# Step sizes at the head of the sample attention, the samples' convolution on GpSimd, and the projection's tail merged into the scan

## The reference, cut to what matters

```python
z, xbc, dt_raw, q, k, v = jnp.split(h @ w_in, SPLIT_EVEN, axis=-1)
xbc, conv_new = causal_dwconv(xbc, conv_buf, conv_w)      # width 4, per channel
xbc = jax.nn.silu(xbc + conv_b)
xs, bmat, cmat = jnp.split(xbc, (D_SSM, D_SSM + SSM_GROUPS * D_STATE), axis=-1)
dt = jax.nn.softplus(dt_raw + dt_bias)                    # step sizes: (tokens, 16 heads)
a = -jnp.exp(a_log)
a_cum = jnp.cumsum(dt * a)                                # within a chunk of 128 tokens
decay = exp(a_cum[l] - a_cum[s])                          # lower triangle
y = (C B^T * decay) (xs * dt) + C h_prev * exp(a_cum)
attn = stick_breaking_attention(q, k, v)                  # causal; samples also see 512 cached keys
out = concat([group_rmsnorm(y * silu(z)), attn]) @ w_out
```

## Time and profile before

| | us |
|---|---|
| median of 3 runs | 1762.31 (1751.34 to 1764.55) |
| the profiled execution, its time | 1760.56 |
| its span (first to last instruction) | 1758.8 |
| PE busy | 1456.4 (83%) |
| VectorE busy | 650.6 (37%) |
| ScalarE busy | 460.8 (26%) |
| GpSimd busy | 213.7 (12%) |

### The profile page before, as it was taken

How to read it: one execution, slowest core, us unless ns; L and a number is a source line. 1 busy time by engine, 2 the same in 40 slices (tenths; PEclk the granted TensorE clock), 3 DMA queues, 4 the chain that set the end, 5 groups by cost and what they waited for, 6 DMA issues and landing times. The chain is left out here.

```text
span 1758.8 us, 25141 instructions
## 1 busy us (share of the span) xinstructions
PE 1456.4 (83%) x10159; PEld 1062.4 (60%) x10159; DVE 650.6 (37%) x1280; ACT 460.8 (26%) x804; POOL 213.7 (12%) x340
## 2 busy tenths in 40 slices
PE   4999789869879687799579988747999839998883
PEld 1999544446669443499445544437999825554443
DVE  3322266552326476662521111144246361111114
ACT  3212265532224352331301100032224130110012
POOL 0000033210000044100011110040000001110104
PEclk8999899879989787799779999968999969999995
DMA  7232497639932510511799999951222299999974
GB/s 295 72 96 73 189 363 262 245 120 348 378 97 72 197 51 0 204 48 49 297 364 387 383 387 398 398 180 47 74 97 78 75 407 347 387 388 394 393 294 157
DMA packets 133592, 399.72 MB, mean 227 GB/s; under 512 B 15842, under 2 KB 67682, under 8 KB 110690
## 3 DMA queue, kind: packets, MB, share of 16 engines
q1 hardware_dynamic: 114370, 359.01, 54.3%
q10 hardware_dynamic: 11488, 21.24, 3.3%
q0 software_dynamic: 7616, 17.84, 3.2%
HBM read 368.72 MB, written 37.19 MB: 231 GB/s over the span
## 5 line engine op out<-in xcount | busy, mean ns | idle before, releaser
L2906 PE MATMUL ex_gups<-ex_gu,ex_he 128*64 128x256 f32 x1728 | 212.6, 402 | 42.3 <-DMA ex_gu<-in_moe_w_up 39.3
L2906 PEld LDWEIGHTS ex_gups<-ex_gu,ex_he 128*64 128x64 f32 x1728 | 127.5, 144 | 111.5 <-DMA ex_gu<-in_moe_w_up 44.2
L2951 DVE TENSOR_TENSOR ex_hid<-ex_sg,ex_gups 128x128 f32<-128x128 f32 x64 | 18.4, 288 | 301.2 <-ACT ex_sg L2975 301.2
L2924 PE MATMUL ex_yps<-ex_dn,ex_hid_t 128*64 128x512 f32 x512 | 123.9, 604 | 0.9 <-issue 0.9
L2817 POOL DMA_INDIRECT ex_hg<-h_rows,route_tok x64 | 60.4, 943 | 433.5 <-PE ex_trps L2896 429.3
L225 PE MATMUL sc_ps<-h_hi,sc_hi 128*128 128x272 f32 x352 | 101.7, 289 | 0.5 <-PEq L3148 0.5
L225 PE MATMUL sc_ps<-hT_r,sc_hi 128*128 128x272 f32 x352 | 100.9, 287 | 0.0
L225 PE MATMUL sc_ps<-h_hi,sc_w_r 128*128 128x272 f32 x352 | 100.7, 286 | 0.0
L2975 ACT ACTIVATE ex_sg<-ex_gups 128x128 f32<-128x128 f32 x64 | 17.8, 278 | 283.9 <-PE ex_gups L2906 283.9
L2965 ACT ACTIVATE ex_yo<-ex_yps 128x512 f32<-128x512 f32 x64 | 38.2, 597 | 184.8 <-PE ex_yps L2924 184.8
L2944 DVE COPY ex_he<-ex_trps 128x512 f32<-128x512 f32 x64 | 44.3, 692 | 63.6 <-PE ex_trps L2896 63.6
(11 more groups left out here) (537 smaller groups left out, 3378.8 us busy)
## 6 DMA issues: line engine op xcount, KB each, us to landing
ex_dn<-in_moe_w_down SPq DMA_DIRECT2D x64, 1024.0 KB, 26.5
ex_gu<-in_moe_w_gate SPq DMA_DIRECT2D x54, 1024.0 KB, 24.6
ex_gu<-in_moe_w_up SPq DMA_DIRECT2D x54, 1024.0 KB, 26.8
ada_rest_w<-in_ada_w SPq DMA_DIRECT2D x40, 1024.0 KB, 6.4
as_pages<-in_cache_kT SPq DMA_DIRECT2D x32, 512.0 KB, 6.6
as_pages<-in_cache_v SPq DMA_DIRECT2D x32, 512.0 KB, 5.4
y_rows<-ex_yo ACTq DMA_DIRECT2D x128, 128.0 KB, 7.0
qkv_w<-in_mix_w_in SPq DMA_DIRECT2D x12, 1024.0 KB, 5.4
```

Source lines behind the costliest of these rows:

```text
L2906: last = nc.tensor.matmul(gu_ps[64 * q:64 * q + 64, :, :], he[n % 2][:, j, :], ex.gu[n % S][:, :, j, q * P:(q + 1) * P], start=(j == 0), s ...
L2924: last = nc.tensor.matmul(y_ps[n % 2][64 * c:64 * c + 64, :], hid_t[:, m * CAP:(m + 1) * CAP], ex.dn[n % S][:, m, c * 512:(c + 1) * 512], ...
L2951: nc.vector.tensor_tensor(hid[:, :], sg[:, :], gu_ps[:, 1, :], ALU.mult).then_inc(done["hid"], 1)
```

## The change

The step sizes move. Their weights (64 KB) are loaded by SP in the prompt attention behind the seventh adaLN load, and split by GpSimd at that stage's end. PE makes the 48 products first thing in the sample attention, ahead of the wait for `qz`, and the five transposes between the halves of the first gate block. VectorE copies the products out behind its first weight split, and makes dt and dA behind its work on the new tokens' weights; ScalarE's exponential and logarithm come between the halves of its copies of z.

The samples' convolution moves to GpSimd, two tiles at a time: one copy, four multiplications and four additions of 128 x 64 elements for each of six steps, five of them in the projection's block, the last in the scan's. The reload of x moves to the projection's start, as SP's third transfer.

The middle block goes. Its last taps and SiLU, the stores of the tail and the last step's sample convolution stand at the head of the scan, among the transposes and sums of chunk 0, which now starts on the eight x tiles that are ready. Unit 0's exponentials come ahead of the four small ones, and its weighing ahead of the multiplication by the decay. `masked(c)` holds the multiplication of C B^T by the triangle, from a PSUM bank of its own (`cb_ps`); the sums use a bank of y. The states' area overlaps `cv_raw`, so their load waits for the last taps and GpSimd's last sample step, behind the store of the tail.

```diff
...
         for t in range(2):
+            if t and between:
+                between(pe)
             f = slice(t * P, (t + 1) * P)
...
+            for part in parts:
+                if part.beside and len(part.beside) > 2:
+                    @block.gpsimd
+                    def _(pool):
+                        part.beside[2](pool)
...
+class StepSizes:
...
+    def load(self, sp):
+        sp.dma_start(self.w[:, :, :], self.k.io["mix_w_in"][:, 2560:2576].rearrange("(k p) n -> p k n", p=P))\
+          .then_inc(self.loaded, 16)
+
+    def divide(self, pool):
+        pool.wait_ge(self.loaded, 16)
+        self.k.nc.gpsimd.tensor_copy(self.hi[:, :, :], self.w[:, :, :]).then_inc(self.split, 1)
+        pool.wait_ge(self.split, 1)
+        self.k.nc.gpsimd.tensor_tensor(self.lo[:, :, :], self.w[:, :, :], self.hi[:, :, :], ALU.subtract)\
+            .then_inc(self.split, 1)
+        pool.wait_ge(self.split, 2)
...
+    def products(self, pe, h_hi):
+        k, nc = self.k, self.k.nc
+        pe.wait_ge(self.split, 2)
+        for h in range(2):
+            cols = slice(h * HALF, (h + 1) * HALF)
+            for j in range(KT):
+                for n, (w, x) in enumerate(((self.hi, h_hi), (self.hi, k.hT_r), (self.lo, h_hi))):
+                    last = nc.tensor.matmul(self.ps[h][0:H, 0:HALF], w[:, j, :], x[:, j, cols],
+                                            start=(j == 0 and n == 0), stop=(j == KT - 1 and n == 2))
+            last.then_inc(self.mm, 1)
...
+    def turn(self, pe):
+        pe.wait_ge(self.out, 2)
+        for i, (a, m) in enumerate(TOK):
+            last = self.k.nc.tensor.transpose(self.turn_ps[0:m, i * H:(i + 1) * H], self.dtT[:, a:a + m],
+                                              self.k.ident[0:H, 0:H])
+        last.then_inc(self.turned, 1)
...
+    def copy_out(self, dve):
+        for h in range(2):
+            dve.wait_ge(self.mm, h + 1)
+            self.k.nc.vector.tensor_copy(self.dtT[:, h * HALF:(h + 1) * HALF], self.ps[h][0:H, 0:HALF])\
+                .then_inc(self.out, 1)
...
+    def vector_part(self, dve):
...
+        own = Chain(dve, self.own_d)
+        own.step(V.memset(u[:, :, :], 0.0))
+        dve.wait_ge(self.turned, 1)
...
+        own.step(V.tensor_tensor(u[:, 0:4, :], turned[:, 0:4, :], bias.unsqueeze(1).to_broadcast([P, 4, H]), ALU.add))
...
+        V.tensor_tensor(u[:, :, :], u[:, :, :], w1[:, :, :], ALU.min).then_inc(self.u_done, 1)
+        dve.wait_ge(self.l_done, 1)
+        V.tensor_scalar(w1[:, :, :], u[:, :, :], 1.0, None, ALU.add).then_inc(self.u_done, 1)
+        dve.wait_ge(self.l_done, 2)
...
+        own.step(V.reciprocal(w1[:, :, :], w1[:, :, :]))
...
+        own.step(V.tensor_tensor(dt_tok[:, :, :], dt_tok[:, :, :], w1[:, :, :], ALU.add))
+        dve.wait_ge(self.rate, 1)
+        own.step(V.tensor_scalar(self.neg_a[:, :], self.neg_a[:, :], -1.0, None, ALU.mult))
+        own.step(V.tensor_tensor(self.dA[:, :, :], dt_tok[:, :, :], self.neg_a[:, :].unsqueeze(1).to_broadcast([P, TT, H]),
+                                 ALU.mult))
+
...
+    def scalar_part(self, act):
+        act.wait_ge(self.u_done, 1)
+        self.k.nc.scalar.activation(self.u[:, :, :], self.u[:, :, :], ACT.Exp).then_inc(self.l_done, 1)
+        act.wait_ge(self.u_done, 2)
+        self.k.nc.scalar.activation(self.ln[:, :, :], self.w1[:, :, :], ACT.Ln).then_inc(self.l_done, 1)
...
                     ada.load(sp, m // KT, m % KT)
+                    if m == 2 * ada.slots:
+                        steps.load(sp)
...
+                steps.divide(pool)
...
+                steps.products(pe, h_hi)
                 pe.wait_ge(s["padded"], 2 * KT)
...
+                    if t == 0:
+                        pe.wait_ge(steps.u_done, 1)
                     pe.wait_ge(s["w"], t + 1)
...
-                    held.products(pe, n, zp_ps, h_hi, k.hT_r)
+                    held.products(pe, n, zp_ps, h_hi, k.hT_r, None if n else steps.turn)
...
                 held.low(dve, 0)
+                steps.copy_out(dve)
...
                 V.tensor_tensor(w_n[:, :, :], w_n[:, :, :], before, ALU.mult).then_inc(s["nw"], 1)
+                steps.vector_part(dve)
...
+                steps.rates(act)
                 held.high(act, 0)
...
-                held.keep(act, 0, zp_ps, zs)
+                held.keep(act, 0, zp_ps, zs, (0,))
+                steps.scalar_part(act)
+                held.keep(act, 0, zp_ps, zs, (1,))
...
-            @block.sync
-            def _(sp):
-                sp.dma_start(k.xT[:, :, :], io["xT"].rearrange("(k p) t -> p k t", p=P)).then_inc(stored, 16)
-                sp.wait_ge(kept_done, 2)
-                sp.dma_start(io["conv_out"], kept[:, :, :]).then_inc(stored, 16)
-                sp.wait_ge(stored, 32)
...
-                pe.wait_ge(split, 2)
...
-                last.then_inc(dt_mm, 1)
-                pe.wait_ge(dt_out, 1)
...
-                taps(dve, STEPS - 1)
-                dve.wait_ge(dt_mm, 1)
-                V.tensor_copy(by_half(dtT[:, :]), dt_ps[:, :, 0:HALF]).then_inc(dt_out, 1)
...
-                for t in range(4):
-                    own.step(V.tensor_tensor(xs if t == 0 else tmp[:, :, :, :], raw_s[:, :, :, t:t + NQ],
-                                             wide(w + t * XT), ALU.mult))
-                    if t:
-                        own.step(V.tensor_tensor(xs, xs, tmp[:, :, :, :], ALU.add))
-                V.tensor_tensor(xs, xs, wide(COLS["conv_b"][0]), ALU.add).then_inc(sample, 1)
-
-                dve.wait_ge(l_done, 1)
...
-                first_tap(act, STEPS - 1)
-                for step in (STEPS - 2, STEPS - 1):
-                    silu(act, step)
-                act.wait_ge(sample, 1)
-                nc.scalar.activation(xc[:, :, TP:T], xc[:, :, TP:T], ACT.Silu).then_inc(act_done, 1)
...
-                nc.scalar.preload_act_table_set("natural_log_exp_and_others")
-                act.wait_ge(u_done, 1)
-                nc.scalar.activation(u[:, :, :], u[:, :, :], ACT.Exp).then_inc(l_done, 1)
...
+    def begin(self, sp):
+        k, held = self.k, self.held
+        sp.dma_start(held.raw[1][:, :, :], held.first[:, :, 256:512]).then_inc(k.w_ready[1], 16)
+        sp.dma_start(self.kept[:, :, :].rearrange("p k t -> p (k t)")[:, 0:XT * NB * 3],
+                     k.io["conv_state"].rearrange("p k b t -> p (k b t)")).then_inc(self.loaded, 16)
+        sp.dma_start(k.xT[:, :, :], k.io["xT"].rearrange("(k p) t -> p k t", p=P)).then_inc(self.x_loaded, 16)
+
...
+    def samples(self, pool, step):
+
+        k, G, own = self.k, self.k.nc.gpsimd, self.pool_own
+        own.eng = pool
+        self.there(pool, step)
+        i = slice(2 * step, 2 * step + 2)
+        xs = self.xc[:, i, TP:T].rearrange("p k (b q) -> p k b q", q=NQ)
...
+        own.step(G.tensor_copy(self.raw_s[:, i, :, 3:3 + NQ], new))
+        for t in range(4):
+            own.step(G.tensor_tensor(xs if t == 0 else self.tmp[:, :, :, :], self.raw_s[:, i, :, t:t + NQ],
+                                     wide("conv_w", t * XT), ALU.mult))
+            if t:
+                own.step(G.tensor_tensor(xs, xs, self.tmp[:, :, :, :], ALU.add))
+        G.tensor_tensor(xs, xs, wide("conv_b", 0), ALU.add).then_inc(self.sample, 1)
+
+    def early_samples(self, pool):
...
+        for step in range(self.STEPS - 1):
+            self.samples(pool, step)
+        pool.wait_ge(self.sample, self.STEPS - 1)
...
+    def keep_tail(self, pool):
+        G = self.k.nc.gpsimd
+        G.tensor_copy(self.kept[:, :, 0:3], self.raw[:, :, TP:TP + 3]).then_inc(self.kept_done, 1)
+        G.tensor_copy(self.kept[:, :, 3:3 + TS], self.raw[:, :, 3 + TP:3 + T]).then_inc(self.kept_done, 1)
+
+    def store(self, sp):
+        sp.wait_ge(self.kept_done, 2)
+        sp.dma_start(self.k.io["conv_out"], self.kept[:, :, :]).then_inc(self.stored, 16)
+
+    def states_may_come(self, sp):
+        sp.wait_ge(self.conv, 6 * self.STEPS)
+        sp.wait_ge(self.sample, self.STEPS)
...
+        assert nc.sbuf_base <= conv.KEPT_AT
+        sst = nc.alloc_sbuf_tensor_at("sst", [P, NB, D], F32, offset=conv.STATES_AT)
...
+        ac_ps = y_ps[1]
...
             def _(sp):
+                conv.store(sp)
+                conv.states_may_come(sp)
                 sp.dma_start(sst[:, :, :], io["ssm_state"]).then_inc(s["sload"], 16)
                 sp.wait_ge(s["zeroed"], 1)
                 for i in range(NE * CAP, NBLK * CAP, P):
...
+                    if c == 0:
+                        pe.wait_ge(conv.smooth, (8, 8, 10)[part])
+                    if c == 4:
+                        pe.wait_ge(conv.smooth_s, 2)
...
-                            pe.wait_ge(s["aexp"], 5)
+                            pe.wait_ge(conv.smooth, XT)
...
+                    elif i == 1:
+                        pe.wait_ge(s["aexp"], 4)
...
-                for part in range(3):
-                    turn(0, part)
+                turn(0, 0)
+                running_sums()
```

(34 more changed lines are left out.)

310 lines of the change are left out of this document (150 added, 160 removed).

## The result

The changed kernel took 1738.54 us (median of 4 runs, 1733.35 to 1741.14) beside 1762.72 for the kernel before (4 runs, 1751.34 to 1764.55): a ratio of 0.9853, 95% interval 0.9828 to 0.9879. Run twice more beside the experiments it gave 0.9879 (0.9859 to 0.9899; medians 1743.52 and 1764.73) and 0.9893 (0.9855 to 0.9932; 1745.77 and 1763.21). So by the medians 24.2, 21.2 and 17.4 us are gone; 18.2 were forecast, and all three times lie in the forecast's range. The profiled executions differ by 20.20 us: 1760.56 and 1740.36.

What follows compares the result with a forecast made beforehand. A serial stretch between projection and scan, no engine near full, was taken to delay the scan. 17.4 + 1.4 - 0.6 = 18.2 us gained: 1742.4 against the profiled execution, 1744.1 against the median; range 1735 to 1756.

Steps and rivals of the forecast that it cites:

- The head: Projection's end to the scan's unit 2: unit 1's broadcast 18.9 us earlier, less for a low clock, gain 17.4 us.
- the low clock: Scan's head, units 1 to 2: PE gaps may drop the clock to half speed, losing 2.5 us, weighed at 0.6.
- The taps' hold: Scan's head: VectorE's six last taps held by small GpSimd operations, 1.8 us taken, between 0 and 2.7.
- the forecast's end of 22.8: Whole kernel, largest gain in us: 18.9 + 1.8 + 2.1, with taps unheld and no cost of the load.
- GpSimd's 54 small operations: Samples' convolution: 45 in the projection cost nothing while PE stays fed; nine in the head, 0.3 us each.
- the rival: Projection and head: GpSimd operations take 0.5 us, not 0.3, and hold VectorE longer; gain 7, time 1755; chance 0.10.
- The sample attention's head: Start of sample attention: moved step-size products leave PE warm, so the gate block ends earlier; +1.4 us, bounds -3 to +2.1.
- the fast case: Sample attention's head: step-size products run at the high clock, are ready at 388.3 and hidden.
- The weights' load in the prompt attention: Prompt attention: 64 KB in 64-byte pieces on SP's queue cost 0.6 us, bounds 0 to -1.5.
- The clock did not stay low through the scan: Slower rival, scan from 617 to 720: clock stays at 0.50, kernel 17 to 35 us slower, 1779 to 1797; chance 0.06.
- the stretch was not covered: Covered rival, before the scan: another chain sets the scan's start, only the front gains, time 1761; chance 0.02.
- the front gave nothing back: Front rival: slow products, gate block 3 us late, load 1.5, low clock in head; gain 12, time 1750; chance 0.12.

Runs made afterwards that it cites:

- the fills: Changed kernel plus matmuls with unread results: 18 in the sample attention and seven in the scan's head, 1742.49 us; nine in the sample attention alone, 1735.96 us.
- three edits: Against the changed kernel, each alone: separate block before the scan, head +7.7 us; samples' convolution on VectorE, +4.3; step sizes at the scan's head, +13.8.

## Why the prediction held, step by step

- **The head, forecast 17.4, measured 19.9.** The mechanism is right: ScalarE's chain from the first taps to unit 1's spreading sets it. ScalarE of the changed kernel in order of time, from the second copy on:

```profile
585.10 0.60 ACT L1977 ACTIVATE x_tok<-ss_trps 128x512 f32<-128x512 f32 x1 [1.20 <-PE ss_trps L1684]
585.59 1.32 ACT L1460 ACTIVATE xc<-xc,small 128x512 f32<-128x512 f32 x2
...
589.35 0.23 ACT L2011 ACTIVATE to_end<-ss_y 128x64 f32<-128x64 f32 x1
...
590.04 1.26 ACT L1986 ACTIVATE ss_mat<-tri_le,dA 128x128 f32<-128x128 f32 x4
```

 Of the 2.5 us between forecast and measurement, 1.5 is the low clock, which I charged with 2.5 x 0.6: between units 1 and 2 lie 4.71 us for 4.61, so it was back in time. It did fall, for unit 0: its two matmuls took 1.91 each, but under ScalarE's SiLU and table load. The other 1.1 lies ahead of unit 1, whose broadcast came 12.09 us after the opening for 13.2: the last SiLU began at 6.3 for 6.8, and the four small ones with the copy of B took 0.7 for 1.1.
- **The taps' hold, forecast 1.8, was 0.26, and the sum hardly felt it.** The taps ended at 584.51 for 585.8, but the last SiLU began only 1.1 us later, behind the second copy, which had waited for PE's slow transposes. The prediction's own links say so too: they put that copy's end at 585.4 (added up, 585.7), so without the hold the sum would have been 0.4 us better at most, not 1.8, and the forecast's end of 22.8 is too high by the rest. That a term seven times too large did so little harm is luck.
- **The rule of the Trainium skill (SBUF — State Buffer, section SBUF: two separate sides)**, by which the shared ports are locked for a whole instruction. First the rows: six taps beside six GpSimd operations took 4.33 us with short ones and 7.64 with long ones. By an estimate from these rows, taking turns for whole instructions would make it 6 x (0.68 + 0.30) = 5.9 and 6 x (0.68 + 0.83) = 9.1. That VectorE is held, and more by longer operations, is as the page says; the size is not, in either case.
- **GpSimd's 54 small operations, forecast to cost nothing in the projection: held.** It took 74.04 us for 74.63; in the experiments it took 73.8 to 75.3 with them and 73.9 to 75.1 without. Each of the beside-taps operations took 0.63 for the forecast 0.3, which was the rival's trigger (0.5 or more), but it was GpSimd that paid: in the projection's last shared step the taps took 4.36 for 4.07. The rival, with its chance of 0.10, is ruled out. The rule on choosing engines (the Trainium skill, GPSIMD Engine Reference, section Engine selection) would have left this work to VectorE: with the whole convolution there the head is 4.3 us longer. GpSimd is the slower engine here too (the last addition of the convolution over all 12 tiles took 0.83 us on it and 0.56 on VectorE), but it was not the one that the head waited for.
- **The sample attention's head, forecast +1.4: 0 was measured.** The 48 products and the small ones ran at full clock, from 385.58 to 392.90, as the fast case had it, and hid. The step that failed is "PE is then warm where it now runs the gate block": the earlier trace rows had 0.67 over 394 to 396, and behind the products PE waited 2.48 us for the weight split and fell just so, here with the sample attention 5 us later:

```profile
394.00:396.00 2.00, 0.63 (x3) 0.63 (x4) 2.00 (x4) 0.00 (x0) 0.00 (x0) 0.73 1.04 418
396.00:398.00 2.00, 2.00 (x10) 2.00 (x10) 1.27 (x9) 0.43 (x2) 0.00 (x0) 0.50 1.01 408
```

 From the prompt attention's end to the gate block's end it is 25.7 us on average of the eight profiles with the products there (24.2 to 26.9, without the fills) and 25.8 in the four without (25.0 to 26.8). The whole stage is 122.5 and 121.9. So within this scatter no cost and no gain of the products is seen.
- **The weights' load in the prompt attention, forecast -0.6: not seen.** The stage took 183.3 us on average with it (eight profiles, 179.3 to 186.1) and 183.6 without (four, 182.4 to 185.0), so a cost of 0.6 can't be told from none.
- **The sum** was 18.2; with 2.5 more for the head, 1.4 less for the sample attention and 0.6 more for the load it is 19.9, and the head is all of it. The total came nearer than the head because the misses partly cancel. The clock did not stay low through the scan (0.88 and 0.83 for 0.88 and 0.77), the stretch was not covered, and the front gave nothing back.

## What to carry to other kernels

A serial head is priced by its longest engine's chain, and each link taken out must be checked for what it leaves PE doing: put back alone, three edits cost 26 us where all of them together had given 20, for each brought back a wait of 5 us or more with PE at the low clock behind it. Small GpSimd operations beside VectorE are nearly free to VectorE and long ones are not, so cut them to the tile rather than merging them (64 and 384 elements are the two lengths tried). Where the stages around an edit scatter by 4 us and more, read the edit's worth at a mark that repeats, as the 17.76 us here did, and not from a handful of totals.

## What the runs showed of the hardware that was not expected

- Filling PE's waits to keep the clock clearly paid in one place of four: nothing was won in the sample attention, where the gate block ended 1.2 and 3.0 us later than on average without a fill, 2.3 us were lost in the changed head, 0.3 won in the old one, and 3.3 won in a wait of 5.09 us.
- The clock behind one and the same wait of 2.3 to 2.7 us is not the same in every execution: the gate block's first half took 6.30 us in two profiles, 7.6 to 7.8 in five and 9.0 in one.
- PE stood still for 2.52 and 1.49 us with its operands ready, both times when it had run eighteen matmuls behind a burst of 128 small ones. Without a fill no row shows such a wait there.
